# A two-block transformer kernel on one core: FFN up-products of 512 columns, MLA products ahead of the norm, and two smaller reorderings

## The reference

```
def swiglu(h, w_gate, w_up, w_down):
    return (jax.nn.silu(h @ w_gate) * (h @ w_up)) @ w_down

def mla_mixer(h, positions, w_down, q_norm, w_uq, kv_norm, w_ukv, w_o):
    down = h @ w_down
    c_q = down[..., :MLA_Q_RANK]                                   # 384
    c_kv = down[..., MLA_Q_RANK:MLA_Q_RANK + MLA_KV_RANK]          # 256
    k_rope = down[..., MLA_Q_RANK + MLA_KV_RANK:]                  # 32
    q = (rmsnorm(c_q, q_norm) @ w_uq).reshape(B_, S, MLA_HEADS, MLA_NOPE_DIM + MLA_ROPE_DIM)
    q_rope = rope(q[..., MLA_NOPE_DIM:], positions)
    kv = (rmsnorm(c_kv, kv_norm) @ w_ukv).reshape(B_, S, MLA_HEADS, MLA_NOPE_DIM + MLA_V_DIM)
    k_rope = rope(k_rope[:, :, None, :], positions)[:, :, 0, :]
    ...
```

## Time and profile before

| | |
|---|---|
| median of 3 runs | 1458.34 us (1457.06 to 1458.89) |
| profiled execution | 1458.99 us, span 1457.2 us |
| mean granted TensorE clock | 0.961 of full speed |
| busy share | TensorE 94%, VectorE 59%, ScalarE 44%, GpSimd 19% |
| chain that ended last | TensorE 85%, VectorE 7%, ScalarE 4% |

### The profile page before, as it was taken

How to read it: one execution, slowest core, us unless ns; L and a number is a source line. 1 busy time by engine, 2 the same in 40 slices (tenths; PEclk the granted TensorE clock), 3 DMA queues, 4 the chain that set the end, 5 groups by cost and what they waited for, 6 DMA issues and landing times.

```text
span 1457.2 us, 28178 instructions
## 1 busy us (share of the span) xinstructions
PE 1364.8 (94%) x10956; PEld 1209.3 (83%) x10956; DVE 855.6 (59%) x1696; ACT 634.9 (44%) x1246; POOL 282.5 (19%) x354
## 2 busy tenths in 40 slices
PE   7899999899899988999998998899999789999998
PEld 6898888789788887999888855899988656799986
DVE  5566666645568876788645345544446555544444
ACT  4344444433144435666445425543334246543343
POOL 0002322211344321132201102111200122111200
PEclk9999999999799999999998969999999989999999
DMA  7312111024321134455555401455454331255552
GB/s 291 116 60 82 67 59 60 31 88 149 117 83 59 59 131 159 175 187 186 181 194 174 162 1 58 145 181 194 173 202 145 115 116 59 87 176 193 180 189 100
DMA packets 26503, 188.87 MB, mean 130 GB/s; under 512 B 2944, under 2 KB 3072, under 8 KB 4128
## 3 DMA queue, kind: packets, MB, share of 16 engines
q1 hardware_dynamic: 25632, 182.51, 35.1%
q0 software_dynamic: 768, 4.92, 1.0%
HBM read 186.37 MB, written 1.05 MB: 129 GB/s over the span
## 4 chain that ended last, share of the span: by engine, by line
PE 85%; DVE 7%; ACT 4%; issue 1%; DVEq 1%; DMA 1%; POOLq 0%; POOL 0%; ACTq 0%; SPq 0%
PE ps L561 48%; PE ps L509 13%; PE ps L809 5%; PE ps L1188 2%; PE ps L660 1%; PE ps L649 1%; PE ps L1050 1%; PE ps L541 1%; PE ps L534 1%; PE ps L774 1%; PE ps L828 1%; PE ps L533 1%; PE ps L908 1%; PE ps L478 1%; DVE mx L1726 1%
## 5 line engine op out<-in xcount | busy, mean ns | idle before, releaser
L561 PE MATMUL ps<-h_hi,w_hi 128*128 128x256 f32 x1208 | 345.5, 286 | 5.0 <-DVE h_lo L1785 5.0
L561 PE MATMUL ps<-h_lo,w_hi 128*128 128x256 f32 x1208 | 344.7, 285 | 0.0
L561 PE MATMUL ps<-h_hi,w_lo 128*128 128x256 f32 x1208 | 344.5, 285 | 0.0
L1815 DVE TENSOR_TENSOR w_lo<-ring,w_hi 128x1024 fp32r<-128x1024 f32 x111 | 139.2, 1254 | 270.5 <-ACT w_hi L1315 270.4
L1315 ACT ACTIVATE w_hi<-ring 128x1024 fp32r<-128x1024 f32 x119 | 126.2, 1060 | 321.5 <-PE ps L561 321.1
L561 PEld LDWEIGHTS ps<-h_hi,w_hi 128*128 128x128 f32 x1208 | 234.8, 194 | 6.6 <-issue 6.6
L561 PEld LDWEIGHTS ps<-h_lo,w_hi 128*128 128x128 f32 x1208 | 234.8, 194 | 0.0
L561 PEld LDWEIGHTS ps<-h_hi,w_lo 128*128 128x128 f32 x1208 | 234.8, 194 | 0.0
L509 PE MATMUL ps<-oT_r,ring_r 128*128 128x256 f32 x512 | 147.3, 288 | 0.0
L1821 DVE TENSOR_TENSOR w_lo<-ring,w_hi 128x1024 fp32r<-128x1024 f32 x111 | 139.7, 1258 | 0.0
L1317 ACT ACTIVATE w_hi<-ring 128x1024 fp32r<-128x1024 f32 x119 | 124.5, 1046 | 0.0
(11 more groups left out here) (406 smaller groups left out, 2786.4 us busy)
## 6 DMA issues: line engine op xcount, KB each, us to landing
ring<-in_weights SPq DMA_DIRECT2D x170, 1024.0 KB, 4.8
arena<-in_aux POOLq DMA_DIRECT2D x1, 2112.0 KB, 12.7
grow<-in_rows POOLq DMA_DIRECT2D x3, 512.0 KB, 3.9
cst<-in_consts SPq DMA_DIRECT2D x1, 1497.5 KB, 14.4
x<-in_x SPq DMA_DIRECT2D x1, 1024.0 KB, 5.0
arena<-in_swbias POOLq DMA_DIRECT2D x1, 1024.0 KB, 7.7
out<-xn SPq DMA_DIRECT2D x4, 256.0 KB, 2.2
sml<-in_small SPq DMA_DIRECT2D x1, 536.0 KB, 5.6
```

The costliest lines, as they stand in the source:

```text
L561: m = pe.matmul(dst, l[a], r[b], start=first and n == 0 and a == b, stop=last and n == len(pairs) - 1 and a == 1)
L1815: dve.tensor_tensor(w_lo[:, half_of(u0, m), WH:], ring[:, (u0 + m) % RING, WH:], w_hi[:, half_of(u0, m), WH:].bitcast(F32), ALU.subtract). ...
```

## The change

It has four parts.

1. `h_hi` and `h_lo` become two halves of one tile `h_both`. In the two FFNs of the second block, `w_hi` meets both in one matmul of 512 columns and `w_lo` meets `h_hi` in one of 256 columns. A tile now takes a whole PSUM bank, a unit two, and VectorE adds the two halves of each bank with a reduction into `uc` before it splits the next weights (`sums`). SiLU and the gating product read `uc`.
2. In MLA the down-projection, multiplied by the norm's gains but not by its roots, is split into `a_hi`, `a_lo`, and the query products use it as split products with 256 columns. The root is multiplied in later: for the queries together with rotation and scale in one table `q_table` (`take_queries`, two heads at once), for keys and values before the products, into `ckv`. The sums of squares are taken per token into 8 columns, GpSimd takes their power, and TensorE spreads them. The weights of these products are split like the others (six more units in `SPLIT`). The last query unit (heads 12 to 15) and half of the values are computed inside the first steps of `heads_pipeline`; the barrier is gone; ScalarE's first splits for the output move from steps 0 and 1 to steps 3 and 4.
3. The rotated keys are copied to the heads by one GpSimd DMA, issued behind the power of the sums.
4. For RWKV pair 0 ScalarE runs `gate_key(0)` ahead of `decays(0)`.

```diff
-                    for tile in range(2):
+                    for tile in range(2 if n_ffn else 0):
+                        bank = ps[2 * j + tile]
+                        for k in range(KT):
+                            if before is not None and tile == 0:
+                                before(k)
+                            hi, lo = [t[:, j % 2, k, tile * P:(tile + 1) * P] for t in w]
+                            pe.matmul(bank[:].rearrange("p (a t) -> p a t", a=2), hi, h_both[:, :, k, :],
+                                      start=k == 0, stop=False)
+                            m = pe.matmul(bank[:, 0:S], lo, h_hi[:, k, :], start=False, stop=k == KT - 1)
...
+                def sums(j, i):
+                    dve.wait_ge(unit_done, u0 + 4 * i + j + 1)
+                    for tile in (1, 0):
+                        bank = ps[2 * (j % 4) + tile]
+                        ins = dve.tensor_reduce(uc[j % 2][:, tile, :], bank[:].rearrange("p (a t) -> p t a", a=2), AX, ALU.add)
+                    ins.then_inc(ff_sum, 1)
...
+            pe.wait_ge(rank_lo, 3)
+            for p, bank in enumerate((6, 7, 3, 0, 1, 2)):
+                if p == 2:
+                    pe.wait_ge(m_sums, 1)
...
+                if p == 4:
+                    pe.wait_ge(m_root, 1)
+                    for c in range(4):
+                        mm = pe.matmul(ps[5][:, c * P:(c + 1) * P], m_stat[:, 2 * c:2 * c + 1].broadcast_to((P, P)),
+                                       ident, start=True, stop=True)
+                    mm.then_inc(m_mm, 1)
...
+            def late_units():
+
+                pe.wait_ge(kv_out, 4)
+                uv_half(1, 0, ps[4], m_mm)
+                yield
+                uv_half(1, 1, ps[5], unit_done)
+                yield
+                yield from uq_pair(6, ps[6])
+                yield from uq_pair(7, ps[7])
...
+            def take_queries(p, bank):
...
+                dve.tensor_tensor(qm[:, 2 * p:2 * p + 2, :], ps[bank][:].rearrange("p (a t) -> p a t", a=2),
+                                  q_table.unsqueeze(1).broadcast_to((P, 2, S)), ALU.mult).then_inc(qv_out, 1)
...
+            pool.tensor_tensor(m_stat, m_stat, stat[:, 16:17].broadcast_to((P, 8)), ALU.pow).then_inc(m_root, 1)
             pool.wait_ge(kr_ready, 1)
-            for h in range(H):
-                pool.tensor_copy(kmT[HD:HD + ROPE, h, :], kr[HD:HD + ROPE])
-            phase_end(pool)
+            pool.dma_start(kmT[HD:P], kr[HD:P].unsqueeze(1).broadcast_to((HD, H, S))).then_inc(kr_all, 16)
...
+            gate_key(0)
             decays(0)
-            gate_key(0)
```

More of the change, by code:

```diff
@@ L632, in out_rows, with heads_pipeline @@
                 pe.drain().then_inc(unit_done, 1)
-            def heads_pipeline(t0, scores, bank_free, p_ready_of, values, fill):
+            def heads_pipeline(t0, scores, bank_free, p_ready_of, values, fill, early=iter(())):
                 for s in range(H + 3):
@@ L641, in heads_pipeline @@
                         scores(s, ps[s % 2]).then_inc(a_scores, 1)
+                    for _ in range(2):
+                        next(early, None)
                     if s >= 6:
@@ L1209, in _, with mla_weights @@
[L1209 to L1218 removed]
+            def mla_weights(m, keys, cols):
+                unit_split("mla", m)
+                return [t[:, (m + 1) % 2, 0:keys * cols].rearrange("p (k c) -> p k c", k=keys) for t in (w_hi, w_lo)]
@@ L1684, in _ @@
[L1684 to L1690 removed]
+            act.wait_ge(unit_done, down + 2)
+            square_rank(2, 1, 0)
+            act.activation(ckv[:, 0, :], ps[1][:, S:2 * S], ACT.Copy, scale=small("g_kv")[:, 0:1])
@@ L2382, in _ @@
-            phase_end(dve)
+            dve.memset(rope_q[0:HD], MLA_SCALE)
+            low_rank_part(2, 1, 0)
+            split_unit(down, "mla", 3)
+            dve.wait_ge(unit_done, down + 3)
+            dve.wait_ge(m_sums, 1)
+            rotated = ps[2][:, S:2 * S]
+            for half_ in range(2):
+                dve.tensor_tensor(rt[HD:HD + ROPE, half_, :], rotated[HD + half_ * ROPE:HD + (half_ + 1) * ROPE],
+                                  rope_t[HD + half_ * ROPE:HD + (half_ + 1) * ROPE], ALU.mult)
@@ new lines, in _ @@
+            dve.drain()
+            for half_ in range(2):
+                ins = dve.tensor_tensor(kr[HD + half_ * ROPE:HD + (half_ + 1) * ROPE], rt[HD:HD + ROPE, 0, :],
+                                        rt[HD:HD + ROPE, 1, :], ALU.add)
+            ins.then_inc(kr_ready, 1)
+            split_unit(down, "mla", 4)
+            split_unit(down, "mla", 5)
+            dve.wait_ge(m_mm, MLA_MM["spread"])
+            dve.tensor_tensor(ckv, ckv, ps[5][:, S:2 * S].unsqueeze(1).broadcast_to((P, 2, S)),
+                              ALU.mult).then_inc(m_norm, 1)
```

304 lines of the change are left out of this document (176 added, 128 removed).

## The result

| | before | after |
|---|---|---|
| median | 1457.70 us (4 runs, 1452.68 to 1458.89) | 1423.82 us (4 runs, 1421.17 to 1425.24) |
| profiled execution: time, span | 1458.99 us, 1457.2 us | 1425.24 us, 1423.4 us |
| mean granted TensorE clock | 0.961 | 0.962 |

The ratio is 0.9767, with a 95% interval of 0.9748 to 0.9786: 34 us less. The forecast was 1422.

A forecast was written before the change was run, and what follows sets the result against it. The prediction took TensorE as the bound, busy for 94% of the span. From 1458.99 us it subtracted 9.0 (FFN), 25.0 (MLA) and 3.4 (first pair), giving 1421.6, said as 1422; range 1411 to 1437.

The forecast's parts named there:

- Term 9.0: Second block's two FFNs: merging matmuls into 512 columns saves 9.0 us, ceiling 9.4, floor 0.
- twice 120.0 is 240.0, so a merge saves 13.3 ns: FFN products: two 256-column matmuls at 120.0 ns pitch become one of 512 at 226.7 ns, in 704 merges.
- Rival C: FFN products: merging does not save the matmul's surplus, FFN gives 0 to 1.8 us, kernel 1430; chance 9%.
- Rival D: FFN sums: the strided PSUM reduction is slow and VectorE bounds the FFN; 1490 at 2.2 us each; chance 4%.
- two handovers without cover: MLA: third query pair's weights ready at 6.8 us, no stall; key weights after the spread, 16.4 against 16.5 us.
- rival B: MLA: bound by weight preparation, not TensorE; 2 us stall per unit, MLA gives 13 us, kernel 1434; chance 15%.
- 2.5 us to give back: MLA up to the heads' early steps: first score 27.5 us sooner, but only 25.0 us taken from this part.
- 9 + 7 fits into 18: Heads' early steps: some 9 us of TensorE work at full clock plus 7.0 us moved products fit into 18.04 us.
- scores of step 6 some 43.5 us behind the down-projection: Sign for the profile after, in MLA's heads: scores of step 6 about 43.5 us after the last down-projection.
- same work, same price: Heads' steps 3 to 6: ScalarE's two splits and GpSimd's four w_lo halves (9.4 us), moved there, cost as before.
- Term 3.4: Start, first pair: copying the key sums ahead of the decays saves 3.4 us, ends 2.0 and 4.5.
- The shift is kept: After the first pair: TensorE is busy almost without a gap, so the 3.4 us won there last.

The follow-up runs named there:

- first profile: The changed kernel itself, its profiled execution, nothing altered: 1425.24 us.
- Norm first: Changed kernel with the MLA sums of squares and the spread of the roots put ahead of the first query pair: ratio 0.9832 to the kernel before.
- second profile: The changed kernel run and profiled again, unaltered, beside follow-up runs: 1425.55 us, ratio 0.9787 to the kernel before.
- early splits: Changed kernel with ScalarE's splits of the first two output units at steps 1 and 3, not 3 and 4: 1421.5 us, ratio 0.9752 to the kernel before.
- late units first: Changed kernel with the last query unit and half of the values computed ahead of the first score: ratio 0.9807 to the kernel before.

## Why the prediction was right, and where its terms were off

**FFN products.** Term 9.0. The two FFNs of the first profile gave 4.6 and 4.4, as summed, but with luck: only two of the ten profiles had the short pitch in both. With the long pitch an FFN gives 2.3. So the merge is worth 4.6 to 9.2, and the kernels with and without it were 5 apart: the step "twice 120.0 is 240.0, so a merge saves 13.3 ns" took pitches of matmuls of one length, one after another, and they held for the alternation of 512 and 256 columns in nine of 20 FFNs only; in the others a merge saves 6.6 ns less, 6.7. Rival C, that nothing is saved, is refuted, and with it, for this stream, the 2.5 ns per merge that would follow from the Trainium skill, "TensorE: Matmul & The Clock Gate", section "Back-to-back issue gap": that rule would have the two FFNs shorter by 1.8 us together, and the long pitch, the nearer of the two, has them shorter by 4.6. What sets the pitch of an FFN stays open; no edit here was made to change it.

**The reductions.** 0.687 us taken, 0.686 measured over 88 of them. They cost TensorE nothing, shown by doubling them. (The cover was summed a little wrong: sums of 1.4 and halves of 2.3 are 3.7 us, not 3.9.) Rival D stays refuted; its break-even of 1.85 us was worked out from durations. With pitches VectorE's unit reaches the 5.76 + 0.65 = 6.4 us of that rival at 0.60 + (6.4 - 3.8) / 2 = 1.9 us, nearly the same, because the two errors (a unit 0.3 us too long, and the whole duration counted for the pitch) nearly cancel.

**MLA to the first score.** Predicted 25.7 us, measured 25.35 twice, at full clock, with all of TensorE's list in it. The two handovers without cover were the right places to name: the third pair waited 0.6 us, where the prediction said "no stall, no cover either"; the keys did not wait. In three of nine profiles the short wait was followed by a low clock that took 1.5 us. That is the part of rival B that is real, 0.6 to 2.1 us out of its 12, and splitting ahead of the rotation removes the 0.6. Norm first costs 10.2 us, so the order of products and norm is worth 10 of the 27.9 us. The other 18 were not taken apart by experiments, except that moving the late units is worth 3.8 at the end; but the two timelines price them. TensorE's two waits of the kernel before, with what it did next:

```profile
1144.44 6.94 PE L1188 MATMUL ps<-arena,ring 128*128 128x256 f32 x18 [6.47 <-DVE arena L2355]
...
1153.42 2.83 PE L1188 MATMUL ps<-arena,ring 128*128 128x256 f32 x12 [0.26 <-issue]
...
1188.07 0.49 PE L1222 MATMUL ps<-arena 96*128 96x128 f32 x2 [1.41 <-DVEq L272]
```

Its queries took 27.6 us (1144.44 to 1172.07). The same eight pairs as split products at 120.0 ns are 17.3: 10.3 less, of which 2.5 are the slow first 18 records (a clock of 0.60 over 1144.44 to 1151.50). As split products the keys are 1.7 us less and the values 1.5, and 7.0 us of products are moved behind the first score. Idle time goes from 7.2 to 0.6 ahead of the products, and from 1.4 to none behind them. Against that stand 0.8 us more for sums and spreads. This adds up to the 27.9, but as a sum of readings: no run changes one of these pieces alone.

**The heads' early steps.** The term was 2.5 us to give back (27.5 down to 25.0); measured 27.9 and 25.1: 2.8. "9 + 7 fits into 18" was right in the busy time at full clock (15.83 us in the second profile) and wrong in the waits: the steps took 20.93 and 19.93. The prediction's own sign, scores of step 6 some 43.5 us behind the down-projection, was missed: they came at 46.3 and 45.3. It didn't fit its term either, for 43.5 would be 27.8 us sooner than before, and 25.0 sooner is 46.3. What the step missed is that TensorE stands behind one small VectorE operation when GpSimd starts a half of `w_lo` beside it. That 25.0 was met all the same is in part luck: beside the wait of 2.53 us, which the sum did not have, these steps ran at a clock of 0.84 or 1.00 where it had been 0.72, which the prediction had only for its upper end of 29. The prediction called the moved splits "same work, same price"; at another place they cost 2.6 us less.

**First pair.** Term 3.4, measured 3.6 on the spot. "The shift is kept" was wrong in eight of twelve profiles, in which a fall of the clock at 270 takes 1.5 back; the edit alone brought 2.2 us in time (0.4 to 3.8).

**What was not in the sum.** Between the attention and the last FFN 1.5 us more. Ten matmuls of the norm (L486) took 2.38 us there, at a clock of 0.50, where the same ones took 1.32 ahead of the first merged FFN and ahead of the last FFN of the kernel before. In the kernel with the early splits they took 1.60, with the late units first 1.32; why the clock is low there was not tested. The down-projection ahead of MLA took 19.5 us instead of 19.0, and only 17.65 in the second profile. In the profiled execution these 1.5 and 0.6 and the first pair's loss (1.6 of the 3.4) come to 3.7 us, and 1421.6 and 1425.24 are 3.6 apart. The median is 1.4 us below that execution.

## What to carry to other kernels

Take costs of back-to-back instructions from the distance of their starts on every engine, VectorE too: its durations overlap by 0.08 us each, and a cost worked out from them was 30 us too high (56 to 65 for 26). Where products are issued ahead of a normalisation, the gain is the idle time and the low clock that would follow it, about half each with the norm first; so look for the small waits that are left, since 0.6 us of idleness, here behind 2.3 us of two-column matmuls, was followed by a loss of 1.5 us more in some executions. When GpSimd's long operations move, look at which small VectorE operation they will run beside, and put them where TensorE has other work.

## What the runs showed of the hardware that was not expected

- The same alternation of 512- and 256-column matmuls runs at 346.6 or 353.3 ns per pair, fixed for a whole FFN and different from one FFN and one execution to the next (nine and eleven of 20).
- At one place of the program TensorE kept its clock in some executions and lost it in others: 36 matmuls took 4.58 or 6.06 us behind the same 20 small sums and 0.59 us of idleness.
- A VectorE operation on 128x2 takes 0.17 us alone and 2.26 us beside a GpSimd operation with two inputs of 1024 elements (2.34 us); it ends when that one does (1167.59 and 1167.56). The Trainium skill, "Advanced Engine Details and Errata", section "VectorE Performance Modes", notes that VectorE's second port is shared with GpSimd, and that GpSimd's instructions and VectorE's two-port ones block each other. The rows agree with such a block, though none shows which ports the operation uses. They give its size: what is left of GpSimd's operation. Two later ones, begun inside one of GpSimd's, take 0.57 and 1.01 us and end with it too (1169.90 and 1169.87; 1175.13 and 1175.10). Sixteen GpSimd copies of 64x256 stretch a 1.22 us operation to 3.06: begun 1.98 us before the last copy ends, it ends 1.08 us behind it.
- A 1 MB DMA from SBUF to SBUF, repeated over 16 heads, takes 9.0 us to landing and doesn't slow VectorE: its halves of a split begun meanwhile (1142.52 and 1144.25) take 1.22 us each, as elsewhere.
